# A SwiGLU feed-forward network in Strassen-style products: seven instead of eight for the remaining pairs, with partial sums formed in PSUM

## What is computed

```python
for i in range(DEPTH):                       # 4
    h = rmsnorm(x, norm_mix[i])
    x = x + mixer_i(h)                       # pool_mix, conv_module, diff attention, pool_mix
    x = x + swiglu(rmsnorm(x, norm_ffn[i]), ffn_w_gate[i], ffn_w_up[i], ffn_w_down[i])

def swiglu(h, w_gate, w_up, w_down):
    return (jax.nn.silu(h @ w_gate) * (h @ w_up)) @ w_down
```

## Time and profile before

| | |
|---|---|
| time, median of 3 runs | 2100.6 us (2098.41 to 2103.76) |
| span of the profiled execution | 2097.1 us |
| TensorE busy | 2036.0 us, 97% |
| VectorE busy | 1407.9 us, 67% |
| ScalarE busy | 967.9 us, 46% |
| GpSimd busy | 684.4 us, 33% |
| HBM traffic | 97 GB/s over the span |

### The profile page before, as it was taken

How to read it: one execution, slowest core, us unless ns; L and a number is a source line. 1 busy time by engine, 2 the same in 40 slices (tenths; PEclk the granted TensorE clock), 3 DMA queues, 4 the chain that set the end, 5 groups by cost and what they waited for, 6 DMA issues and landing times.

```text
span 2097.1 us, 41264 instructions
## 1 busy us (share of the span) xinstructions
PE 2036.0 (97%) x16836; PEld 1960.9 (94%) x16836; DVE 1407.9 (67%) x1950; ACT 967.9 (46%) x1590; POOL 684.4 (33%) x493
## 2 busy tenths in 40 slices
PE   8999999999899999999999989999999999999999
PEld 7999999997499899999999869999999999999999
DVE  5974687468669746874566645874687369737862
ACT  5542344365455423443677744542344354423432
POOL 4540343169325403431111123441333125303521
PEclk9999999999999999999999989999999999999999
DMA  5332333244222323433532343232333322333332
GB/s 183 89 93 84 100 111 87 85 122 119 61 78 79 94 84 101 111 87 90 176 121 77 121 156 92 71 101 84 98 102 97 111 56 81 95 90 108 102 91 82
DMA packets 350017, 208.19 MB, mean 99 GB/s; under 512 B 9897, under 2 KB 340553, under 8 KB 349812
## 3 DMA queue, kind: packets, MB, share of 16 engines
q1 hardware_dynamic: 345988, 198.26, 32.6%
q0 software_dynamic: 3472, 6.96, 1.0%
q10 hardware_dynamic: 384, 0.55, 0.1%
HBM read 194.53 MB, written 8.60 MB: 97 GB/s over the span
## 4 chain that ended last, share of the span: by engine, by line
PE 79%; DVE 8%; POOL 5%; ACT 4%; issue 3%; DMA 1%; SPq 0%; ACTq 0%; POOLq 0%; DVEq 0%
PE acc L685 40%; PE acc L885 13%; PE acc L914 9%; PE pair L885 6%; POOL conv L2586 4%; PE bank L885 3%; DVE w_lo L1855 2%; POOL w_sum L2545 1%; PE pair L1099 1%; ACT w_hi L1331 1%; PE bank L1119 1%; DVE xt_lo L2005 1%; DVE xn L1996 1%; DMA hist_rows<-in_state_pool 1%; PE pair L1074 1%
## 5 line engine op out<-in xcount | busy, mean ns | idle before, releaser
L1855 DVE TENSOR_TENSOR w_lo<-raw,w_hi 128x768 fp32r<-128x768 f32 (+1 forms) x252 | 326.5, 1295 | 233.0 <-ACT w_hi L1331 226.4
L1331 ACT ACTIVATE w_hi<-raw 128x768 fp32r<-128x768 f32 (+1 forms) x252 | 232.7, 923 | 429.6 <-PE acc L685 426.2
L685 PE MATMUL acc<-h_hi,w_hi 128*128 128x260 f32 x1408 | 399.1, 283 | 0.0
L685 PE MATMUL acc<-h_lo,w_hi 128*128 128x260 f32 x1408 | 398.3, 283 | 0.0
L685 PE MATMUL acc<-h_hi,w_lo 128*128 128x260 f32 x1408 | 397.6, 282 | 0.0
L685 PE MATMUL acc<-xin_hi,w_hi 128*128 128x260 f32 x1152 | 332.4, 289 | 7.7 <-DVE w_lo L1855 6.4
L685 PE MATMUL acc<-xin_hi,w_lo 128*128 128x260 f32 x1152 | 325.4, 282 | 0.0
L685 PE MATMUL acc<-xin_lo,w_hi 128*128 128x260 f32 x1152 | 325.1, 282 | 0.0
L2545 POOL TENSOR_TENSOR w_sum<-raw 128x512 f32<-128x512 f32 x56 | 97.2, 1735 | 637.7 <-DMA raw<-in_ffn_w_up 546.3
L685 PEld LDWEIGHTS acc<-h_hi,w_hi 128*128 128x128 f32 x1408 | 265.3, 188 | 0.3
L685 PEld LDWEIGHTS acc<-h_hi,w_lo 128*128 128x128 f32 x1408 | 265.0, 188 | 0.0
(11 more groups left out here) (455 smaller groups left out, 5417.0 us busy)
## 6 DMA issues: line engine op xcount, KB each, us to landing
raw<-in_ffn_w_gate SPq DMA_DIRECT2D x88, 512.0 KB, 4.0
raw<-in_ffn_w_up SPq DMA_DIRECT2D x88, 512.0 KB, 5.2
raw<-in_ffn_w_down SPq DMA_DIRECT2D x64, 384.0 KB, 3.4
raw<-in_ffn_w_down SPq DMA_DIRECT2D x64, 320.0 KB, 3.2
raw<-in_attn_w_qkv SPq DMA_DIRECT2D x24, 512.0 KB, 3.8
raw<-in_conv_w_in SPq DMA_DIRECT2D x16, 512.0 KB, 4.1
raw<-in_conv_w_out SPq DMA_DIRECT2D x8, 512.0 KB, 4.1
in_mix<-in_cache_k SPq DMA_DIRECT2D x8, 512.0 KB, 5.2
```

The lines of the kernel that those rows point to most:

```text
L685: last = pe.matmul(acc[:, b, 0:HALF], w[:, w_tile * P:(w_tile + 1) * P], v[:, h * HALF:(h + 1) * HALF], start=start and t == 0, stop=stop ...
L1331: act.activation(w_hi[n.slot(2)][:, 0:cols], raw[:, q.slot(4), 0:cols], ACT.Copy).then_inc(split_hi, 1)
L1855: dve.tensor_tensor(w_lo[n.slot(2)][:, 0:cols], raw[:, raw_of(n).slot(4), 0:cols], w_hi[n.slot(2)][:, 0:cols].bitcast(F32), ALU.subtract). ...
```

## The change

1. **All S.** ROUNDS_OF and `plain_pair` go. A layer has 18 pairs in seven products behind its four plain pairs, 7 in the first half and 11 in the second. The eighth activation block (plain_hi, plain_lo) goes with it.
2. **Partial sums in PSUM.** Products 0, 2, 4 and 6 add into one bank, that of `pair[J % 2]`, in turn: the bank holds product 0, then 0+2, 0+2+4 and 0+2+4+6. Products 1, 3 and 5 have banks of their own. The order of products and their weight sums are changed to fit. ScalarE copies the bank after products 0, 2 and 4 (begun0 to begun2, begun_ok, L1500 of the changed kernel), and TensorE waits for each copy before it adds the next product: products 2, 4 and 6 wait for begun_ok.
3. **Joins.** VectorE adds one begun to each of products 1, 3 and 3, and with_t1 to 5, 260 columns each, and makes h in two parts, the second straight from PSUM.
4. **Weight sums.** GpSimd keeps w_sum[0] and w_sum[2]; VectorE makes w_sum[1] (`w_sum_2`, behind product 5 for the pair after the next) and w_sum[3] (`w_sum_4`, behind product 0 for the next pair). w_sum[1] waits for GpSimd's first sum. Both kinds have semaphores of their own.
5. **h's parts.** `h_high` and `h_low` of a pair move into product 0 of the next pair.
6. **Warming.** The six steps on a constant become 40 matmuls of 512, 256, 128, 260 and 384 columns on w_hi x xin_hi, behind a wait for the split of conv_out's first weights.

```diff
-ROUNDS_OF = ("SSOSSOS", "SSSOSSSOSSS")
...
+PAIRS_OF = (range(0, FH - PLAIN), range(FH - PLAIN, 2 * FH - PLAIN))
+PAIRS = 2 * FH - PLAIN
...
-        BLOCK_BANK = tuple(acc[:, b, 0:HALF] for b in (0, 2, 1, 3)) + (pair[:, 1, 0:HALF], pair[:, 0, 0:HALF], bank6[:, 0:HALF])
...
+        W_SUM = (None, None, 1, 0, 2, 3, None)
+        def block_bank(J, b):
+            return (pair[:, J % 2, 0:HALF], bank6[:, 0:HALF], None, acc[:, 2, 0:HALF], None, acc[:, 3, 0:HALF], None)[b if b % 2 else 0]
...
-                            last = pe.matmul(BLOCK_BANK[b], w[:, cols], v[:, k, :], start=k + t == 0, stop=k == 3 and t == 2)
+                            last = pe.matmul(block_bank(J, b), w[:, cols], v[:, k, :], start=k + t == 0 and b in (0, 1, 3, 5),
+                                             stop=k == 3 and t == 2, skip_group_check=b % 2 == 0)
                     last.then_inc(blk_done, 1)
-                def seven_blocks(J, tiles_done, f):
+                def seven_blocks(j, tiles_done):
+                    J = PAIRS * layer + j
+                    if j >= 2:
+                        pe.wait_ge(h_ready, FT * layer + PLAIN + j - 1)
+                    block(J, 0)
                     if J:
-                        pe.wait_ge(first_ok, J)
-                    if f is None:
-                        pe.wait_ge(evacuated, tiles_done - 1)
-                    else:
-                        pe.wait_ge(sg_ready, FT * layer + f)
-                    block(J, 0)
+                        pe.wait_ge(joined, 4 * J - 3)
+                    block(J, 1)
+                    pe.wait_ge(begun_ok, 3 * J + 1)
+                    block(J, 2)
                     pe.wait_ge(evacuated, tiles_done)
-                    for b, joins in ((1, 1), (2, 1), (3, 2), (4, 4), (5, 4), (6, 5)):
-                        if J:
-                            pe.wait_ge(joined, 5 * J - 5 + joins)
-                        block(J, b)
-                def plain_pair(n, J):
...
+                    if J:
+                        pe.wait_ge(joined, 4 * J - 1)
+                    block(J, 3)
+                    pe.wait_ge(begun_ok, 3 * J + 2)
+                    block(J, 4)
+                    if J:
+                        pe.wait_ge(joined, 4 * J)
+                    block(J, 5)
+                    pe.wait_ge(begun_ok, 3 * J + 3)
+                    block(J, 6)
...
-                for _ in range(6):
-                    keep_warm(acc[:, 3, :], const[:, C_DIST:C_DIST + SEQ])
                 u, m0 = UNIT["conv_out"], TILE["conv_out"]
+                pe.wait_ge(split_hi, u + 1)
+                for k in range(KT):
+                    pe.matmul(acc[:, 3, :], w_hi[0][:, k * P:(k + 1) * P], xin_hi[:, k, 0:SEQ], start=True, stop=True)
...
+                        act.wait_ge(w_summed_dve if b in (2, 5) else w_summed_pool, 2 * J + (1 if b < 4 else 2))
...
+                        if b in (0, 2, 4):
+                            if J:
+                                act.wait_ge(joined, 4 * J - 3 + b // 2)
+                            act.activation(begun[b // 2][:], pair[:, J % 2, 0:HALF], ACT.Copy).then_inc(begun_ok, 1)
+                        if b == 0 and j not in (0, PAIRS_OF[1][0]):
+                            h_high(f - 1)
...
+                def w_sum_2(j):
+                    q, J = raw_of_pair(layer, j), PAIRS * layer + j
+                    dve.wait_ge(landed[q.slot(4)], (q.turn(4).v + 1) * 16)
+                    dve.wait_ge(w_summed_pool, 2 * J + 1)
+                    dve.tensor_tensor(w_sum[:, 1, :], w_sum[:, 0, :], raw[:, q.slot(4), 0:512], ALU.subtract).then_inc(w_summed_dve, 1)
+                def w_sum_4(j):
+                    q, J = raw_of_pair(layer, j), PAIRS * layer + j
+                    dve.wait_ge(w_summed_dve, 2 * J + 1)
+                    dve.tensor_tensor(w_sum[:, 3, :], raw[:, q.slot(4), 512:1024], w_sum[:, 1, :], ALU.subtract).then_inc(w_summed_dve, 1)
...
+                        if b == 1:
+                            dve.wait_ge(begun_ok, 3 * J + 1)
+                            dve.tensor_tensor(silu2[:, 0:HALF], gate_0, begun[0][:], ALU.add).then_inc(joined, 1)
...
+                            dve.tensor_tensor(with_t1[:], only_t1, begun[1][:], ALU.add).then_inc(joined, 1)
...
+                            dve.tensor_tensor(up_1, only_t1, begun[2][:], ALU.add).then_inc(joined, 1)
...
+                            dve.tensor_tensor(silu2[:, HALF:T], gate_1, with_t1[:], ALU.add).then_inc(joined, 1)
...
+                            dve.tensor_tensor(h2[:, HALF:T], up_1, silu2[:, HALF:T], ALU.mult)
+                            dve.tensor_tensor(h2[:, 0:HALF], block_bank(J, 6), silu2[:, 0:HALF], ALU.mult).then_inc(h_ready, 1)
                         ahead(b)
+                        if not last and b == 0:
+                            w_sum_4(j + 1)
+                        if b == 0 and j not in (0, PAIRS_OF[1][0]):
+                            h_low(f - 1)
+                        if b == 5 and j + 2 <= PAIRS_OF[j >= PAIRS_OF[1][0]][-1]:
+                            w_sum_2(j + 2)
...
+                        pool_e.wait_ge(blk_lo, 7 * J - 3)
+                    pool_e.tensor_tensor(w_sum[:, 0, :], up[:, 0:512], up[:, 512:1024], ALU.add).then_inc(w_summed_pool, 1)
+                    pool_e.wait_ge(landed[q.slot(4)], (q.turn(4).v + 1) * 16)
                     if J:
                         pool_e.wait_ge(blk_lo, 7 * J - 2)
-                    pool_e.tensor_tensor(w_sum[:, 0, :], up[:, 0:512], up[:, 512:1024], ALU.add).then_inc(w_summed, 1)
-                    pool_e.wait_ge(w_summed, 4 * J + 1)
-                    pool_e.tensor_tensor(w_sum[:, 1, :], w_sum[:, 0, :], gate[:, 0:512], ALU.subtract).then_inc(w_summed, 1)
-                    pool_e.tensor_tensor(w_sum[:, 2, :], gate[:, 0:512], up[:, 0:512], ALU.subtract).then_inc(w_summed, 1)
-                    if J:
-                        pool_e.wait_ge(blk_lo, 7 * J)
-                    pool_e.wait_ge(w_summed, 4 * J + 2)
-                    pool_e.tensor_tensor(w_sum[:, 3, :], gate[:, 512:1024], w_sum[:, 1, :], ALU.subtract).then_inc(w_summed, 1)
+                    pool_e.tensor_tensor(w_sum[:, 2, :], gate[:, 0:512], up[:, 0:512], ALU.subtract).then_inc(w_summed_pool, 1)
```

236 lines of the change are left out of this document (78 added, 158 removed).

## The result

The changed kernel takes 2116.8 us (median of 4 runs, 2112.7 to 2123.4) beside 2099.5 us before: ratio 1.008, 95% interval 1.0051 to 1.0109. Run again beside other executions of the kernel before it was 2118.5 against 2101.6 (1.0075, 1.0051 to 1.0098). The forecast was 2107 with a range of 2076 to 2127. The likeliest case's sign and its two chains came out; its sum is 10 us too low.

What follows compares the result with a forecast made beforehand. TensorE, busy 97% of the span, was taken as the bound. First half 80.7 us (80.4 before) and second 116.0 (114.6) gave +1.7 us a layer, +7 in all on 2100.6: 2107 us, range 2076 to 2127.

Steps and rivals of the forecast that it cites:

- The likeliest case: Whole kernel: 2107 us, slower by 1.7 us a layer; own range 2096 to 2118, chance 0.45.
- its two chains: ScalarE's copy behind h_hi at each layer's opening, and VectorE's h-to-h cycle in steady pairs, take back the matmul gain.
- Matmuls: Sixteen pairs go from 96 to 84 matmuls, 10.09 us a pair; gain with gap and clock at most 54 us.
- Opening: First pair of each layer: TensorE's product 2 waits for ScalarE's copy behind h_hi, a stall of 6.7 us.
- Slow clock: Behind the gap in each layer's first pair: slower matmuls cost 1.5 us, bounds 0 and 3.
- Steady pairs: VectorE's cycle from h to h: 8.9 plus 2.0 us of GpSimd waits; halves lose 1.9 and 5.0 us.
- The forecast's other reading: VectorE blocked for the whole GpSimd sum: 1.29 us for each wait, total 2118 instead of 2107.
- (a): Faster: GpSimd's sums fall beside joins or VectorE's idle time, cycle 9.9 us; 2077 to 2084 us, chance 0.25.
- (b): Slower: weights land later or the wait is whole, cycle 11.1 to 11.3 us; 2118 to 2128 us, chance 0.15.
- (c): Slower: TensorE's short repeated waits in steady pairs bring the clock down; 2125 to 2160 us, chance 0.07.
- (d): At each layer's opening the copy comes early and TensorE doesn't stall; 2047 to 2075 us, chance 0.05.
- Warming: Before conv_out, 40 matmuls instead of six steps: taken as 0 us, bounds 0 and +1, once.

Runs made afterwards that it cites:

- experiment 1: Changed kernel, but at each layer's opening ScalarE copies the first pair's bank ahead of the last plain pair's h_hi; 2103.7 us.
- experiment 2: Changed kernel with GpSimd's two weight sums cut to 8 columns in every pair but the first of a layer, waits kept; 2079.0 us.
- experiment 3: Changed kernel with all four weight sums of a pair on VectorE, none on GpSimd; 2092.5 us.
- experiment 8: Changed kernel with all four weight sums of a pair on GpSimd, as in the kernel before; 2123.3 us.
- experiment 6: Changed kernel with 52 extra matmuls on a free bank between products 1 and 2 of each layer's first pair; 2105.8 us.
- edits 1, 3 and 4: Changed kernel with first-pair copies ahead of h_hi, all sums on VectorE, h's parts later (this last alone 2091.9 us); together 2066.4 us.

## Why the forecast came out as it did

**Matmuls.** A pair at full pace is 10.07 us (10.09 forecast). Right.

**Opening.** h at 102.71 (102.3 forecast), the first copy at 103.98, product 2 at 104.40 (104.0), a gap of 6.5 us in all four layers (6.7). The copy queued behind h_hi is the cause: with it ahead (experiment 1) the gap is 0.6. Here the forecast's working held to the step; of the one or two holds that it left open one came. The gap follows what stands ahead of h on VectorE: 5.3 us in experiment 2, 7.5 in 3, 8.9 in 8.

**Slow clock.** Forecast 1.5 us, bounds 0 and 3. Products 2 and 3 took 109.76 - 104.40 = 5.4 us, and 3.0 in experiment 6, so 2.4 (2.1 in layer 2). This term was under-sized: I took the value of a gap of 3.9 us for one of 6.5. With it the first pair of a layer takes 19.4 us on average where the sum had 18.3.

**Steady pairs.** Forecast 8.9 us of work and handing over and 2.0 of waits, 10.9 in all; measured 8.8, 1.9 and 10.71. Of the three operations that the forecast named for the two holds, the subtraction and VectorE's own sum were held, and half of h was not (0.42 us at 306.02). The onset, three free pairs and the last pair free, is what the trace shows. Experiment 2 takes the waits away and leaves 10.07 everywhere. The second halves were forecast at 116.0 and took 115.9 to 116.6. In the second halves one or two pairs take 11.2 instead of 10.7, which the sum doesn't have; in layer 0 it is the case of a landing of 6 us, the upper bound of the forecast.

**The shared ports.** The trace agrees with the rule on the shared port pair (the Trainium skill, "SBUF — State Buffer", section "SBUF: two separate sides") as to who is held. The holds measured 0.8 to 1.1 us behind sums of 1.3. They are shorter than a sum because VectorE's operation starts when the sum has run for some time already; it ends 0.54 and 0.55 us after the sum (304.39 after 303.85, 306.10 after 305.55), so these rows don't speak against blocking to the sum's end. The forecast's other reading, 1.29 us for each wait and 2118 in total, isn't what the rows show, although the median comes close to that number; it comes there by other terms.

**The sum.** Per layer I had 80.7 + 116.0 = 196.7, and got 81.8 + 116.2 = 198.0: 1.3 us a layer, nearly all of it in the first pair. But I had read the stretches of before as 4 x 195.0 = 780.0, and they are 781.4. Of the change itself the forecast had +6.8 us in the stretches and the profiles show +10.6, so 4 of the 10 us are there. Another 4 are outside the stretches, for which the forecast had zero: 1.6 us in the attention layer and 1.8 in the last pool mixer in the first profile, and 3.7 and 1.7 in the second, against the first profile of before (against its other two profiles the attention layer is 4.2 us longer in the first and 6.3 in the second). The last 2 are between profiled execution and median.

**Rivals.** (a), holds that fall beside the joins, needs pairs of 10.07 to the end; there are none past the third until GpSimd's sums are cut away. (b), a slower cycle of 11.1 to 11.3, gave 2118 to 2128, and the measured median lies within 2 us of it, but the steady cycle is 10.7; a late landing makes single pairs of 11.2 and no more. (c), a clock that falls in the steady pairs, isn't there (1.00 in the second halves). (d), no stall at the opening, fell.

**Warming.** Zero forecast, zero measured in the convolution itself.

## What to carry to other kernels

A partial sum that must be copied out before the next product can start puts the copying engine's whole queue on TensorE's path: before such an edit, look at what stands ahead of the copy in that queue at the opening, not only in the steady state. Where VectorE and GpSimd share work, count what a GpSimd operation costs VectorE in waits (here 0.8 to 1.1 us for each of 1.3), and count only waits that lie in the cycle. Where that is over what the same operation costs on VectorE (0.60 us here), GpSimd's help is a loss: moving the last two sums (experiment 3) gained 24 us, while moving the first two, which the change did, gained nothing in the steady pairs (experiment 8). And an edit that takes a wait away is worth only the distance to the next wait on the same chain: edit 1 removed most of 6.5 us of idling and the slow clock behind it in each layer and gained 3.0 to 3.3; edits 1, 3 and 4 gave 13, 24 and 25 us alone and 50 together.
